# Compression of the sparse mixer with the token blocks stationary, and three modulation chunks folded during attention on GpSimd

## The chip, the cores and the metric

The kernel runs on one core of a Trainium2 chip. The metric is the device time of one execution in microseconds (us), as the median of several runs. The engines are TensorE (PE, and PEld for its weight loads), VectorE (DVE), ScalarE (ACT), GpSimd (POOL) and SyncE (SP), which issues the transfers.

## The reference, cut to what matters

The model has a two-layer transformer (the first layer with a sparse mixer, the second with differential attention), a gated delta network, and a mixture of many small experts. The change touches the sparse mixer of the first layer alone, and the modulation vector computed beside it.

```python
mod = jax.nn.silu(c) @ ada_w[i] + ada_b[i]          # c: 1024 values, mod: 6 * 1024
...
def nsa_compress(t, pos_emb, w1, w2):
    S = t.shape[2]
    ncmp = (S - NSA_CMP_LEN) // NSA_CMP_STRIDE + 1  # (256 - 32) // 16 + 1 = 15
    idx = np.arange(ncmp)[:, None] * NSA_CMP_STRIDE + np.arange(NSA_CMP_LEN)[None, :]
    blocks = t[:, :, idx] + pos_emb
    hid = jax.nn.silu(jnp.einsum('bgnld,lde->bgne', blocks, w1))
    return jnp.einsum('bgne,ed->bgnd', hid, w2)
```

For each of two key heads g there are 15 blocks of 32 tokens with 64 features d, every second block half over the one before. A block is flattened to 2048 values and multiplied by w1 (32 x 64 x 256), once for the keys and once for the values. The compressed keys are then scored against the queries, masked and put through a softmax whose rows are weighted by gates. The compressed attention is one of three branches that `sparse_attention` adds up.

## The kernel before, in words

The kernel is a row of stages. Each is a block in which every engine has its own queue of instructions, written out by hand, with semaphores between them; a barrier and the clearing of the stage's semaphores stand between two blocks. The stages around the change are `turn` (transposes of z, the projected tokens), `compress`, `sparse_attention` and `project` (the output projection).

**Weights.** w1 lies in SBUF as [128 partitions, 2 (key, value), 16, 256], fp32, 4 MB. The 128 partitions hold two tokens: 64 features of an even token l in the lower half, the same of the odd token behind it in the upper half, so that one matmul contracts two tokens. It comes in four transfers of 1 MB, two for the keys, issued by `turn` (L579) behind the positions `pos_t` and w2, and two for the values, issued by `compress` (L989).

**Compression (`compress`).** TensorE turns the tokens of both heads into `pt`, twice, into the lower and the upper 64 partitions (L1007). VectorE copies them to `tok_t` (L1074) and builds `blk` by adding the positions (L1080), even tokens for the lower half, odd ones for the upper, four additions each for key and value. TensorE then keeps a 128x128 piece of w1 stationary and moves the 30 blocks (2 heads x 15) through it: 2 (key, value) x 2 (halves of the 256 hidden values) x 16 (pairs of tokens) matmuls (L1015). An fp32 matmul of this kind shows as two records. ScalarE applies Silu from PSUM (L1053). TensorE multiplies by w2 (L1022, L1026); VectorE copies the compressed keys and values out (L1088, L1089); TensorE scores (L1035); VectorE scales and masks (L1093), takes the maximum (L1098) and subtracts it (L1099); ScalarE takes Exp (L1056); VectorE sums and weighs (L1102 to L1106); TensorE transposes the probabilities in four quarters (L1044) and VectorE copies each out (L1109).

**Modulation beside it (`Modulation`).** `mod` is built up in 24 chunks of 1 MB, one after another over several stages. A fold is one VectorE operation of 128x2048 (L178): acc = w * silu(c) + acc. Chunks 14 to 19 are loaded in this stage (L163) through two slots; the load of the third and of each later one waits until a fold has freed its slot. VectorE folds four behind the building of the blocks, one behind the copy of the compressed values, and one between the subtraction and the sum. GpSimd clears a row (L152) and does nothing else.

**Attention (`sparse_attention`).** Twelve pairs of heads go through a pipeline: TensorE scores (L1153), VectorE scales and masks from PSUM (L1204) and takes two maxima (L1209), ScalarE takes Exp and sums (L1239), VectorE takes the reciprocal (L1216), for eight pairs multiplies it by gates (L1220), and multiplies the rows in two pieces (L1222), TensorE transposes (L1163), ScalarE copies (L1247), and TensorE multiplies by the values (L1174, L1178). SyncE starts the first two tiles of the output weights at the stage's beginning (L217). GpSimd has no part.

```python
            fold(0, 4)
            dve.wait_ge(small, 1)
            ...
            dve.tensor_tensor(sc[:], sc[:], mx[:].unsqueeze(3).broadcast_to(wide), ALU.subtract).then_inc(shifted, 1)
            fold(5, 6)
            dve.wait_ge(exped, 1)
```

## Time and profile before

| what | value |
|---|---|
| median of 3 runs | 2252.08 us (2250.52 to 2254.69) |
| profiled execution, its own time | 2255.32 us |
| its span in the profile | 2253.5 us |
| compression, as a stretch of it | 137.3 to 190.7 us |
| attention of the sparse mixer | 190.7 to 236.0 us |
| busy: PE, DVE, ACT, POOL | 89%, 70%, 44%, 6% |

All times of the timeline are microseconds from the start of the span. The span is one execution; the time of the run around it is 1.8 us longer. A duration of a matmul record holds its latency, so neighbouring records overlap, and the pace is told by the time of many divided by their number. The granted clock (PEclk) is given in shares of full speed.

### The profile page before, as it was taken

The page shows a single profiled execution, that of the slowest core. Times are in us where ns is not written, and L with a number is a line of the kernel's source. Part 1 is how long each engine was busy: PE and PEld are TensorE (multiplying, and loading weights), DVE is VectorE, ACT ScalarE, POOL GpSimd, SP SyncE. Part 2 cuts the span into 40 slices and gives each one's busy share as a digit, 9 for nine tenths or more (in the row PEclk, how much of TensorE's full clock was granted, in tenths as well). Part 3 has the DMA queues.
Part 4 walks back from the last instruction along what each step waited for, and adds up shares of the span by engine and source line. Part 5 has one row for each costly group of instructions (what it writes and reads, how often), then busy time and mean ns, then how long its engine had stood idle before and what let it go on. Part 6 is the DMA issues. An engine that isn't in the chain of part 4 may idle for free. (4 is left out here: it accounts for less than half of the span.)

```text
span 2253.5 us, 40848 instructions
## 1 busy us (share of the span) xinstructions
PE 2013.6 (89%) x16472; PEld 1805.2 (80%) x16472; DVE 1570.8 (70%) x2622; ACT 1002.6 (44%) x1669; POOL 125.6 (6%) x109
## 2 busy tenths in 40 slices
PE   8877799988779996998788888899899999999996
PEld 4875599968559894878777868899899998888885
DVE  3658778867559886776566565589977776667665
ACT  2515444335553343323344553445456665454453
POOL 1000000000230001530000300000000000000000
PEclk9967999989789998998899988999999999999998
DMA  7672578835137882314000025477555555777775
GB/s 262 229 165 82 196 291 319 310 119 187 59 134 282 304 299 70 119 57 151 1 4 4 2 86 189 150 230 216 181 170 176 176 176 196 240 242 244 241 241 179
DMA packets 185264, 393.24 MB, mean 174 GB/s; under 512 B 14826, under 2 KB 130154, under 8 KB 173546
## 3 DMA queue, kind: packets, MB, share of 16 engines
q1 hardware_dynamic: 166642, 373.83, 49.1%
q10 hardware_dynamic: 18434, 16.79, 2.2%
q8 instruction: 131, 2.15, 0.4%
q14 instruction: 57, 0.47, 0.1%
HBM read 371.17 MB, written 19.40 MB: 173 GB/s over the span
## 5 line engine op out<-in xcount | busy, mean ns | idle before, releaser
L1319 ACT CAST experts_v_hi<-peer_v 128x1024 fp32r<-128x1024 f32 x128 | 134.3, 1050 | 175.8 <-PE experts_py L1309 174.7
L1516 PE MATMUL ffn_pa<-all_h_hi,ffn_u_hi 128*128 128x256 f32 x704 | 199.4, 283 | 7.1 <-DVE ffn_u_lo L1581 7.0
L1305 PE MATMUL experts_py<-experts_v_hi,experts_c_hi 128*128 128x512 f32 x512 | 200.4, 391 | 5.3 <-DVE experts_c_lo L1350 5.3
L1306 PE MATMUL experts_py<-experts_v_lo,experts_c_hi 128*128 128x512 f32 x512 | 200.1, 391 | 0.0
L1517 PE MATMUL ffn_pa<-all_h_lo,ffn_u_hi 128*128 128x256 f32 x704 | 198.2, 282 | 0.0
L1518 PE MATMUL ffn_pa<-all_h_hi,ffn_u_lo 128*128 128x256 f32 x704 | 198.2, 281 | 0.0
L1309 PE MATMUL experts_py<-experts_v_hi,experts_c_lo 128*128 128x512 f32 x512 | 158.4, 391 | 0.0
L3148 PE MATMUL table_pa<-all_h_hi,table_u_hi 128*128 128x256 f32 x512 | 151.1, 295 | 7.6 <-DVE table_u_lo L3116 7.6
L1344 DVE TENSOR_TENSOR experts_v_lo<-peer_v,experts_v_hi 128x1024 fp32r<-128x1024 f32 x128 | 155.9, 1218 | 0.6 <-ACT experts_v_hi L1319 0.6
L3070 PE MATMUL route_pa<-all_h_hi,route_u_hi 128*128 128x256 f32 x512 | 146.5, 286 | 8.8 <-DVE route_u_lo L2955 8.8
L3071 PE MATMUL route_pa<-all_h_lo,route_u_hi 128*128 128x256 f32 x512 | 145.7, 285 | 0.0
L3149 PE MATMUL table_pa<-all_h_lo,table_u_hi 128*128 128x256 f32 x512 | 145.7, 285 | 0.0
L3150 PE MATMUL table_pa<-all_h_hi,table_u_lo 128*128 128x256 f32 x512 | 145.7, 285 | 0.0
L3072 PE MATMUL route_pa<-all_h_hi,route_u_lo 128*128 128x256 f32 x512 | 145.6, 284 | 0.0
L1516 PEld LDWEIGHTS ffn_pa<-all_h_hi,ffn_u_hi 128*128 128x128 f32 x704 | 134.3, 191 | 10.9 <-DVE ffn_u_lo L1581 9.3
L1517 PEld LDWEIGHTS ffn_pa<-all_h_lo,ffn_u_hi 128*128 128x128 f32 x704 | 134.4, 191 | 1.6 <-issue 0.2
L1518 PEld LDWEIGHTS ffn_pa<-all_h_hi,ffn_u_lo 128*128 128x128 f32 x704 | 134.3, 191 | 0.0
L833 PE MATMUL proj_psum<-proj_w_hi,all_h_hi 128*128 128x256 f32 (+1 forms) x384 | 112.2, 292 | 18.4 <-DVE proj_w_lo L845 18.4
L1350 DVE TENSOR_TENSOR experts_c_lo<-experts_coef,experts_c_hi 128x256 fp32r<-128x256 f32 x128 | 54.4, 425 | 106.3 <-ACT experts_c_hi L1325 106.3
L1581 DVE TENSOR_TENSOR ffn_u_lo<-ffnw_u,ffn_u_hi 128x2048 fp32r<-128x2048 f32 (+1 forms) x50 | 101.2, 2034 | 38.7 <-ACT ffn_u_hi L1553 38.7
L1553 ACT CAST ffn_u_hi<-ffnw_u 128x2048 fp32r<-128x2048 f32 (+1 forms) x50 | 84.3, 1702 | 94.7 <-DMA ffnw_u<-in_ffn_columns 92.7
L3116 DVE TENSOR_TENSOR table_u_lo<-table_u,table_u_hi 128x1024 fp32r<-128x1024 f32 x64 | 78.5, 1227 | 63.7 <-ACT table_u_hi L3175 63.7
(586 smaller groups left out, 5828.9 us busy)
## 6 DMA issues: line engine op xcount, KB each, us to landing
peer_v<-in_peer_v SPq DMA_DIRECT2D x128, 512.0 KB, 3.4
ffnw_u<-in_ffn_columns SPq DMA_DIRECT2D x44, 1024.0 KB, 7.9
ffn_ada_w<-in_ada_w SPq DMA_DIRECT2D x40, 1024.0 KB, 5.4
route_u<-in_peer_u SPq DMA_DIRECT2D x64, 512.0 KB, 3.8
table_u<-in_peer_u SPq DMA_DIRECT2D x64, 512.0 KB, 3.3
ffnw_v<-in_ffn_rows SPq DMA_DIRECT2D x44, 512.0 KB, 8.7
peer_kept<-hid_kept SPq DMA_DIRECT2D x128, 128.0 KB, 3.4
l1w_w<-in_diff_w_in SPq DMA_DIRECT2D x12, 1024.0 KB, 5.1
```

The lines of the kernel that those rows point to most:

```text
L1305: pe.matmul(py[:, 2 * t + n, :], c_hi[:, b, part], v_hi[:, r, cols], start=start, stop=False)
L1306: pe.matmul(py[:, 2 * t + n, :], c_hi[:, b, part], v_lo[:, r, cols], start=False, stop=False)
L1309: last = pe.matmul(py[:, 2 * t + n, :], c_lo[:, b, part], v_hi[:, r, cols], start=False, stop=stop)
L1344: dve.tensor_tensor(v_lo[:, r, :], feed_v.slot(i), v_hi[:, r, :].bitcast(F32), ALU.subtract).then_inc(v_split, 1)
L1516: pe.matmul(out, u_hi[:, b, cols], h_hi[:, c, :], start=(c == 0), stop=False)
L1517: pe.matmul(out, u_hi[:, b, cols], h_lo[:, c, :], start=False, stop=False)
L1518: last = pe.matmul(out, u_lo[:, b, cols], h_hi[:, c, :], start=False, stop=(c == KT - 1))
L3070: pe.matmul(out, u_hi[:, b, cols], h_hi[:, c, :], start=(c == 0), stop=False)
L3071: pe.matmul(out, u_hi[:, b, cols], h_lo[:, c, :], start=False, stop=False)
L3148: pe.matmul(out, u_hi[:, b, cols], h_hi[:, c, :], start=(c == 0), stop=False)
L3149: pe.matmul(out, u_hi[:, b, cols], h_lo[:, c, :], start=False, stop=False)
L3150: last = pe.matmul(out, u_lo[:, b, cols], h_hi[:, c, :], start=False, stop=(c == KT - 1))
```

## The change

- The blocks are the stationary operand now, padded from 30 to 32 columns, and w1 moves, 256 columns at a time. The 16 token pairs are dealt out over four groups of 32 columns of TensorE (`l % 4`), each of which collects a partial sum in its own 32 partitions of PSUM.
- ScalarE copies the four partial sums to `part`, and two matmuls against `stack` (four 32x32 unit matrices, one below another) add them and turn the result, hidden values to the partitions. Silu reads that.
- The upper 64 partitions of `tok_t` hold the tokens shifted by one, so that both halves are read with the same pattern: two additions of 128 partitions take the place of four of 64. `pos_t` is shifted in the same way by its transfer.
- w2 is loaded behind w1 instead of ahead of it, with a semaphore of its own. Silu's table is loaded by an activation of one column (`warm`).
- VectorE's work on the gates stands behind the building of the blocks, and ScalarE makes the last four copies instead of VectorE.
- Of the six modulation chunks three stay in the compression: the first on VectorE behind the copy of the compressed values, the second on GpSimd, the third on VectorE at the very end. Chunks 17 to 19 are loaded in attention, ahead of the output weights in SyncE's queue, and folded by GpSimd. A fold on GpSimd is two operations, a multiplication in place and an addition.

```diff
+    def fold_in_two(self, pool, chunk):
+        at = chunk - self.first
...
+        pool.wait_ge(self.w_loaded[at % 2], 16 * (at // 2) + 16)
+        pool.tensor_tensor(w, w, silu_c[:, c:c + 1].broadcast_to([P, AW]), ALU.mult).then_inc(self.weighed, 1)
+        self.halfway += 1
+        pool.wait_ge(self.weighed, self.halfway)
+        if at and c:
+            pool.wait_ge(self.folded, at)
...
+        pool.tensor_tensor(acc, acc, w, ALU.add).then_inc(self.folded, 1)
 def compress(...)
         @block.sync
-            for to, of, arrived in w1_rest:
+            for to, of, arrived in transfers:
         @block.gpsimd
+            pool.memset(warm[:], 0.0).then_inc(warm_ready, 1)
             beside.zero(pool)
+            beside.fold_in_two(pool, halves[1])
         @block.tensor
-                pe.wait_ge(blk_ready, 4 * (kv + 1))
+                pe.wait_ge(blk_ready, 2 * (kv + 1))
                 pe.wait_ge(w1_loaded[kv], 32)
+                for l in range(L):
+                    rows = slice(l % 4 * GROUP, (l % 4 + 1) * GROUP)
+                    last = pe.matmul(ph[rows, kv, 0:CMP_HIDDEN], blk[:, kv, l, :], w1[:, kv, l, :], start=(l < 4),
+                                     stop=(l >= L - 4))
+                last.then_inc(e_sum, 1)
+                pe.wait_ge(part_ready, kv + 1)
                 for e in range(2):
-                    for l in range(L):
-                        last = pe.matmul(ph[:, kv, e * N:(e + 1) * N], w1[:, kv, l, e * P:(e + 1) * P],
-                                         blk[:, kv, l, :], start=(l == 0), stop=(l == L - 1))
-                    last.then_inc(e_sum, 1)
+                    last = pe.matmul(pt[kv][:, e * N:(e + 1) * N], part[:, kv, e * P:(e + 1) * P], stack[:, 0:N],
+                                     start=True, stop=True)
+                last.then_inc(joined, 1)
         @block.scalar
+            act.wait_ge(warm_ready, 1)
+            act.activation(warm[:], warm[:], ACT.Silu).then_inc(warmed, 1)
             for kv in range(2):
-                act.wait_ge(e_sum, 2 * (kv + 1))
-                act.activation(hid[:, kv].rearrange("p e n -> p (e n)"), ph[:, kv, 0:2 * N],
+                act.wait_ge(e_sum, kv + 1)
+                act.copy(part[:, kv, :], ph[:, kv, 0:CMP_HIDDEN]).then_inc(part_ready, 1)
+                act.wait_ge(joined, kv + 1)
+                act.activation(hid[:, kv].rearrange("p e n -> p (e n)"), pt[kv][:, 0:2 * N],
                                ACT.Silu).then_inc(hid_ready, 1)
...
+            for quarter in range(4):
+                act.wait_ge(p_turned, quarter + 1)
+                act.copy(pc_t[:, 2 * quarter:2 * quarter + 2, :].rearrange("n h s -> n (h s)"),
+                         pt[quarter % 2][0:NCMP, :]).then_inc(p_half, 1)
 def sparse_attention(...)
+        beside = Modulation(nc, k, st, *ada)
         @block.sync
         def _(sp):
+            for chunk in range(ada[2], ada[3]):
+                beside.load(sp, chunk)
             for feed in feeds:
                 feed.begin(sp)
+
+        @block.gpsimd
+        def _(pool):
+            for chunk in range(ada[2], ada[3]):
+                beside.fold_in_two(pool, chunk)
```

Where the folds stand is seen in the order of instructions. VectorE, compression, before: L178 is a fold, `cmp_kc_t` and `l0b_vc` are the compressed keys and values, `cmp_sc` the scores.

```order
L1080 TENSOR_TENSOR cmp_blk<-cmp_tok_t,l0b_pos_t 64x240 x4
L178 SCALAR_TENSOR_TENSOR main_mod<-cmp_ada_w,main_silu_c,main_mod 128x2048 x4
L1088 COPY cmp_kc_t<-cmp_pk 64x15 x2
L1089 COPY l0b_vc<-cmp_pv 15x128
L178 SCALAR_TENSOR_TENSOR main_mod<-cmp_ada_w,main_silu_c,main_mod 128x2048
L1093 SCALAR_TENSOR_TENSOR cmp_sc<-cmp_psc,main_cmp_mask 128x120 x2
L1098 TENSOR_REDUCE cmp_mx<-cmp_sc 128x16
L1099 TENSOR_TENSOR cmp_sc<-cmp_sc,cmp_mx 128x240
L178 SCALAR_TENSOR_TENSOR main_mod<-cmp_ada_w,main_silu_c,main_mod 128x2048
L1102 TENSOR_REDUCE cmp_sm<-cmp_sc 128x16
```

The same place of VectorE's queue now:

```order
L1113 TENSOR_TENSOR cmp_blk<-cmp_tok_t,l0b_pos_t 128x8x30 x2
L1118 TENSOR_SCALAR l0b_gates<-l0b_gates 128x48
L1119 RECIPROCAL l0b_gates<-l0b_gates 128x48
L1123 COPY cmp_kc_t<-cmp_pk 64x15 x2
L1124 COPY l0b_vc<-cmp_pv 15x128
L178 SCALAR_TENSOR_TENSOR main_mod<-cmp_ada_w,main_silu_c,main_mod 128x2048
L1128 SCALAR_TENSOR_TENSOR cmp_sc<-cmp_psc,main_cmp_mask 128x120 x2
L1133 TENSOR_REDUCE cmp_mx<-cmp_sc 128x16
L1134 TENSOR_TENSOR cmp_sc<-cmp_sc,cmp_mx 128x240
L1136 TENSOR_REDUCE cmp_sm<-cmp_sc 128x16
```

The four folds ahead of the key copy are gone, one is left between that copy and the scores, and none stands between the subtraction and the sum.

GpSimd, compression and attention, now (before, the clearing of `main_mod` was the only operation here; `ada_w` is the chunk in its slot):

```order
L1019 MEMSET cmp_warm 128x1
L152 MEMSET main_mod 128x2048
L188 TENSOR_TENSOR cmp_ada_w<-cmp_ada_w,main_silu_c 128x2048
L195 TENSOR_TENSOR main_mod<-main_mod,cmp_ada_w 128x2048
L72 UNCONDITIONAL_BRANCH
L68 ISA x24
L1179 UNCONDITIONAL_BRANCH
L188 TENSOR_TENSOR attn_ada_w<-attn_ada_w,main_silu_c 128x2048
L195 TENSOR_TENSOR main_mod<-main_mod,attn_ada_w 128x2048
```

One pair of operations stands in the compression; in attention the last two rows stand there three times.

## Rows read from the trace of the kernel before

**Rows 1.** Busy time of each engine by stretch, both stages; granted clock as PEclk

```profile
core 0: us, PE busy (x) PEld busy (x) DVE busy (x) ACT busy (x) POOL busy (x), PEclk, DMA share, GB/s
146.70:160.60 13.90, 13.86 (x66) 13.89 (x66) 0.53 (x1) 0.00 (x0) 0.00 (x0) 0.50 1.12 248
160.60:174.30 13.70, 13.62 (x64) 13.49 (x64) 8.88 (x4) 0.26 (x2) 0.00 (x0) 0.50 0.75 234
174.30:190.70 16.40, 8.90 (x48) 6.62 (x48) 10.79 (x18) 1.87 (x3) 0.00 (x0) 0.50 0.24 74
190.70:236.00 45.30, 35.42 (x280) 22.89 (x281) 37.56 (x80) 33.58 (x117) 0.00 (x0) 0.93 0.12 47
```

**Rows 2.** Timeline of the compression: start, duration, engine, line, operation, count

```profile
137.31 1.97 PE L1007 MATMUL cmp_pt<-all_ident,l0b_z 128*64 128x128 f32 x32 [0.83 <-PEq L72]
...
146.74 27.48 PE L1015 MATMUL cmp_ph<-cmp_blk,l0b_w 128*128 128x30 f32 x128 [7.46 <-DMA l0b_w<-in_cmp_w]
...
162.99 2.35 DVE L178 SCALAR_TENSOR_TENSOR main_mod<-cmp_ada_w,main_silu_c,main_mod 128x2048 f32<-128x2048 f32 x1 [0.57 <-DMA cmp_ada_w<-in_ada_w]
...
174.26 0.22 ACT L1053 ACTIVATE cmp_hid<-cmp_ph 128x60 f32<-128x60 f32 x1 [13.43 <-PE cmp_ph L1015]
...
176.16 0.37 DVE L1088 COPY cmp_kc_t<-cmp_pk 64x15 f32<-64x15 f32 x2 [2.30 <-PE cmp_pv L1026]
...
176.90 3.62 PE L1035 MATMUL cmp_psc<-cmp_kc_t,l0b_zt 128*128 128x30 f32 x16 [0.78 <-DVE l0b_vc L1089]
...
181.62 0.41 DVE L1099 TENSOR_TENSOR cmp_sc<-cmp_sc,cmp_mx 128x240 f32<-128x240 f32 x1
...
181.95 2.34 DVE L178 SCALAR_TENSOR_TENSOR main_mod<-cmp_ada_w,main_silu_c,main_mod 128x2048 f32<-128x2048 f32 x1
...
182.06 0.40 ACT L1056 ACTIVATE cmp_sc<-cmp_sc 128x240 f32<-128x240 f32 x1 [6.28 <-DVE cmp_sc L1099]
...
186.04 3.69 PE L1044 MATMUL cmp_pt<-all_ident,cmp_sc 128*15 128x128 f32 x16 [5.52 <-DVE cmp_sc L1106]
...
189.77 0.68 DVE L1109 COPY l0b_h_t<-cmp_pt 15x512 f32<-15x512 f32 x1 [0.18 <-PE cmp_pt L1044]
```

**Rows 3.** DMA into l0b_w, and issues of 120 to 192

```profile
L989 SPq DMA_DIRECT2D l0b_w<-in_cmp_w x2: 533/1342/2152, 137.3 to 137.8; - x2
DMA to landing us min/median/max: 2.1/14.0/19.4
...
cmp_ada_w<-in_ada_w SPq DMA_DIRECT2D x6, 1024.0 KB, 5.7
```

**Rows 4.** Timeline of TensorE at the end of attention

```profile
230.71 0.65 PE L1174 MATMUL attn_po<-attn_pt,l0b_z 128*64 128x256 f32 x4
```

**Rows 5.** GpSimd's groups by line: busy, mean ns of one

```profile
L1817 POOL TENSOR_TENSOR diff_w_lo<-diff_w,diff_w_hi 128x1024 fp32r<-128x1024 f32 x8 | 18.9, 2361 | 0.1
...
L2628 POOL TENSOR_TENSOR dnrec_faded<-dnrec_state,dna_exp_last 128x512 f32<-128x512 f32 x8 | 8.3, 1042 | 0.0
```

**Rows 6.** Timeline of the recurrence, VectorE and GpSimd

```profile
1270.91 1.04 POOL L2628 TENSOR_TENSOR dnrec_faded<-dnrec_state,dna_exp_last 128x512 f32<-128x512 f32 x1
...
1271.56 0.94 DVE L2685 TENSOR_TENSOR dnrec_rhs<-dnrec_bv,dnrec_rhs 128x512 f32<-128x512 f32 x1
```

**Rows 7.** Two lines of VectorE in the recurrence: min/median/max ns

```profile
L2685 DVE TENSOR_TENSOR dnrec_rhs<-dnrec_bv,dnrec_rhs x12: 691/814/943, 1266.2 to 1304.5; 128x512 f32<-128x512 f32 x12
...
L2682 DVE TENSOR_TENSOR dnrec_rhs<-dnrec_pks,dna_k_scale x12: 680/690/692, 1265.4 to 1303.7; 128x512 f32<-128x512 f32 x12
```

**Rows 8.** Timeline of VectorE in attention, one round

```profile
203.81 0.95 DVE L1204 SCALAR_TENSOR_TENSOR attn_sc<-attn_ps,main_causal 128x768 f32<-128x768 f32 x1
204.80 1.01 DVE L1209 TENSOR_REDUCE attn_nm<-attn_sc 128x2 f32<-128x256 f32 x2
205.73 0.17 DVE L1216 RECIPROCAL attn_sm<-attn_sm 128x4 f32<-128x4 f32 x1
205.93 1.02 DVE L1222 TENSOR_TENSOR attn_sc<-attn_sc,attn_sm 128x256 f32<-128x256 f32 x2
```

More of the change, by code:

```diff
@@ L1060, in _ @@
             step = InOrder(dve, dve_done)
-            def fold(first, last):
-                for n in range(first, last):
-                    beside.fold(dve, halves[n])
-            dve.wait_ge(gate_e, 1)
-            step(dve.tensor_scalar(gates[:], gates[:], 1.0, None, ALU.add))
             step(dve.memset(kc_t[:], 0.0))
-            step(dve.reciprocal(gates[:], gates[:]))
-            dve.wait_ge(small_loaded, 48)
+            step(dve.memset(blk[:, :, :, N:GROUP], 0.0))
+            step(dve.tensor_reduce(stack[:], k["ident"][:].rearrange("p (j n) -> p n j", n=GROUP), AX.X, ALU.add))
+            dve.wait_ge(small_loaded, 32)
             half = L // 2
@@ L1073, in _ @@
                 dve.wait_ge(turned, kv + 1)
-                step(dve.tensor_copy(tok_t[:, kv].rearrange("d g s -> d (g s)"), pt[kv][:]))
-                for odd, rows in enumerate(sides):
-                    steps = tok_t[rows, kv].rearrange("d g (m l o) -> d l g m o", l=half, o=2)[:, :, :, :, odd]
-                    places = pos_t[rows, kv].rearrange("d (l o) -> d l o", o=2)[:, :, odd]
-                    for m in range(2):
-                        at = slice(m * half, (m + 1) * half)
-                        dve.tensor_tensor(blk[rows, kv, at, :].rearrange("d l (g n) -> d l g n", g=G),
-                                          steps[:, :, :, m:m + NCMP],
-                                          places[:, at].unsqueeze(2).unsqueeze(3).broadcast_to([HEAD, half, G, NCMP]),
-                                          ALU.add).then_inc(blk_ready, 1)
-            fold(0, 4)
+                for g in range(G):
+                    last = dve.tensor_copy(tok_t[:, kv, g, 0:S - 1], pt[kv][:, g * S:(g + 1) * S - 1])
+                step(last)
+                steps = tok_t[:, kv].rearrange("d g (m l o) -> d l g m o", l=half, o=2)[:, :, :, :, 0]
+                places = pos_t[:, kv].rearrange("d (l o) -> d l o", o=2)[:, :, 0]
+                for m in range(2):
+                    at = slice(m * half, (m + 1) * half)
+                    dve.tensor_tensor(blk[:, kv, at, 0:N].rearrange("d l (g n) -> d l g n", g=G),
+                                      steps[:, :, :, m:m + NCMP],
+                                      places[:, at].unsqueeze(2).unsqueeze(3).broadcast_to([P, half, G, NCMP]),
+                                      ALU.add).then_inc(blk_ready, 1)
+            dve.wait_ge(gate_e, 1)
+            step(dve.tensor_scalar(gates[:], gates[:], 1.0, None, ALU.add))
+            step(dve.reciprocal(gates[:], gates[:]))
             dve.wait_ge(small, 1)
@@ L1089, in _ @@
             dve.tensor_copy(vc[:].rearrange("n g d -> n (g d)"), pv[0:NCMP, 0:G * HEAD]).then_inc(kv_ready, 1)
-            fold(4, 5)
+            beside.fold(dve, halves[0])
             dve.wait_ge(scored, 1)
@@ L1099, in _ @@
             dve.tensor_tensor(sc[:], sc[:], mx[:].unsqueeze(3).broadcast_to(wide), ALU.subtract).then_inc(shifted, 1)
-            fold(5, 6)
             dve.wait_ge(exped, 1)
@@ L1106, in _, with sparse_attention @@
             dve.tensor_tensor(sc[:], sc[:], sm[:].unsqueeze(3).broadcast_to(wide), ALU.mult).then_inc(p_ready, 1)
[L1107 to L1113 removed]
+            beside.fold(dve, halves[2])
+def sparse_attention(nc, k, z, zt, pc_t, vc, gates, o_t, feeds, ada):
     pairs = []
```

52 lines of the change are left out of this document (30 added, 22 removed).

## The prediction

> **What bounds the kernel now.** I read the page for the whole first (VectorE 70% busy, TensorE 89%), but the change touches two stages only, so the question is what ends last in each of them. Everything outside the two I leave as it is: after them the next stage starts at a barrier, and what is due there (the first two tiles of the output weights) lands early in either kernel.
>
> The table by stretches [rows 1] shows the first stage, the compression, from 137.3 to 190.7. From 146.7 to 174.3 TensorE is busy throughout (13.86 of 13.90, 13.62 of 13.70) at a granted clock of 0.50, that is at 1.2 GHz; it had been idle before, waiting for weights. The other engines have next to nothing to do there. From 174.3 to 190.7 nobody is full: 16.4 us of a chain from engine to engine. In the attention stage VectorE is busy for 37.56 of 45.3, nearly without a gap once it has started; TensorE (35.42) and ScalarE (33.58) follow it. GpSimd does nothing in either (0.00).
>
> The timeline [rows 2] gives the chain of the compression. The 128 records of the block product start at 146.74, when the first half of the weights is there, and end at 174.22: 27.48/128 = 0.215 us each. Silu ends at 174.48, the key and value copies start at 176.16, the scores end at 176.90+3.62 = 180.52, the subtraction of the maximum at 182.03. Exp is done at 182.46, but VectorE is in a fold until 184.29. The transposes start at 186.04 and the last copy ends at 190.45. The second half of the weights is not waited for: it was issued at about 137.8 and landed up to 19.4 later, 157.2 [rows 3], while the product was still on the first.
>
> **The change, part by part.** All in us of the profiled execution.
>
> *The weights.* The 128 KB of w2 go behind the 4 MB of w1 instead of ahead of them. That advances w1 by at most the 2.1 that w2 took to land [rows 3] and at least by nothing; I take 1.3, so the second half lands at 155.9. The total ahead of the modulation chunks is unchanged, so the second of these is there at 162.99 as before [rows 2]. What was hidden, the landing at 155.9, is now on the path.
>
> *The product.* Per key or value there are now 16 matmuls of 32 stationary columns and 256 moving ones: 32 records over four column groups. The nearest row is the value product of attention: 4 records of 256 moving columns over two column groups take 0.65 at the full clock [rows 4]. With 0.21 a record side by side that is two steps and the latency of the last; one after another it would be 0.85 and the latency. So two groups do run at once, and they keep it up: L1007's 32 records of 128 columns, at the full clock too, take 1.97 [rows 2], two per 0.12. For four I take 32/4 = 8 steps of 0.43 at the half clock (the engine again comes from a wait) plus 0.2: 3.6. Bounds: 1.8 at the full clock; 6.9 if only two groups run at once; 13.7 if none do. The second product ends at 155.9+3.6 = 159.5.
>
> *The joining.* New on the path: a ScalarE copy of 128x256 (as the 128x240 Exp, 0.40 [rows 2]), four records of 0.215 and their latency (1.1), then Silu (0.22) and some 0.1 of hand-over. Silu ends at 161.4 instead of 174.48: 13.1 earlier. The table load for Silu is hidden in both kernels under the wait for the weights. VectorE's block building also gets shorter, and the clearing of pads and the `stack` reduction are added, but all of it ends before 146; it costs nothing while the weights are the later.
>
> *The tail.* The fold between the subtraction and the sum goes: the sum waits for Exp (182.46) instead of the fold (184.29), and about 1.7 is gained. The four last copies go to ScalarE, as short as they were. The last fold on VectorE runs beside the transposes and needs a chunk that is loaded once the first fold is done: at 166 to 170, so it lands 5.7 later [rows 3], by 175.5 at the latest, and VectorE is then just done with the probabilities or not yet. If this were all, the stage would end at 190.45-13.1-1.7 = 175.65, **14.8 earlier**.
>
> *GpSimd beside VectorE.* This decides the sign. A fold on GpSimd is two tensor_tensor of 128x2048. The trace has it at 1.04 for 512 elements a partition and 2.36 for 1024 [rows 5]. Four times the first is 4.2, the line through both gives 5.0; I take 4.5. (Trainium skill, "GPSIMD Engine Reference", section on elementwise cycle accounting: 4497 ns for this length; the rows allow it.)
>
> Does it disturb VectorE? In the recurrence VectorE's L2685 reads two SBUF tensors. It takes 0.69 alone and 0.94 when it starts under a GpSimd tensor_tensor [rows 6, 7]: GpSimd ends at 1270.91+1.04 = 1271.95, L2685 starts at 1271.56 and ends at 1272.50, that is 0.55 after GpSimd let go. L2682, with one input in PSUM and one in SBUF, stays at 0.68 to 0.69 through the same overlaps. So an operation with two SBUF inputs seems to stand still until the GpSimd one is done. (Trainium skill, "SBUF — State Buffer", "Who interferes with whom": a two-SBUF-input VectorE instruction and a GpSimd one that reads SBUF hold each other off for the whole instruction. The trace agrees on 0.4 us of it; no row shows a wait of 4 us. By this rule the change costs time; by shared bandwidth it would not.)
>
> In the compression the second chunk lands at 162.99 and GpSimd multiplies until 167.5. VectorE would start its fold (two SBUF inputs) at 163.7; it is held to 167.5 and ends at 169.8. The scores were ready at 167.4. GpSimd's addition waits for that fold, runs to 174.3, and holds the subtraction (two SBUF inputs), due at 170.9. The subtraction ends at 174.8 instead of 169.0: **+5.8**. Had VectorE come first, it would be +5.1. The stage ends at 181.4, 9.0 earlier.
>
> In attention one round of VectorE is 3.06: mask 0.95, two reductions 1.01, reciprocal 0.17, all with at most one SBUF tensor, then two multiplications by the row factors, 1.03, with two [rows 8]. The first chunk lands 5.7 after the stage begins [rows 3], and then six operations of 4.5 stand in GpSimd's queue almost without a gap. If VectorE gets both multiplications between two of them, a round lasts 4.5+1.0 = 5.5, +2.5; six times 15, and 1 more for the first, which arrives just ahead of a pair. Where GpSimd slips in between the two, VectorE waits the full 4.5. Ends: 14 (always the pair, 4.2 each) and 25 (always between, 4.9 each); I take **+18**, nearer the lower end because the two multiplications follow each other at once. TensorE and ScalarE have slack in a stretched round, at the half clock too. SP's order is load, load, load after the first fold, then the output weights: these start some 15 after the stage begins and are needed after 60.
>
> Sum: -14.8 +5.8 +18 = **+9.0**. Against the profiled execution's own 2255.3 that is 2264; it lies 3.2 above the median of the three runs, so against that median I forecast 2261.
>
> The places in the order are the ones shown ahead: the folds that leave VectorE's queue, and the pairs in GpSimd's.
>
> **Rivals.**
> *No hold.* GpSimd and VectorE run beside each other without loss. For it: L2685 is one kind of row, with 0.4 of overlap at most, and most operations under GpSimd keep their time [rows 7]. Against it: the end of L2685 follows the end of GpSimd's. Then only the 14.8 count: 2252.1-14.8 = 2237.3, faster. It decides as soon as the hold per GpSimd operation is under about 1.5.
> *A slowdown, no standstill.* A 0.25 longer L2685 in 0.39 of overlap is also a rate of a third. Then the fold loses some 2.5 and the subtraction 0.8, and in attention five rounds lose 2 each: -14.8+3.3+10 = -1.5, 2250.6, within 0.2%.
> *The column groups run one after another.* 13.7 instead of 3.6 after the landing: the end of the chain is only 3 earlier, GpSimd's multiplication is then over before VectorE's fold, about 2 of hold are left: -3.0-1.7+2+18 = +15, 2267. The two groups of [rows 4] speak against it.
> *GpSimd always gets in between the multiplications*: +16, 2268; part of the forecast's range. With the cheap end everywhere it is -14.8+5.1+14 = +4, 2256.
>
> **Numbers.** What a measurement of this kernel can tell from no change is about 0.2%, 4.5 us. Forecast 0.59, no hold 0.21, slowdown 0.12, groups in turn 0.08. Of the forecast's 0.59 some 0.03 fall within 0.2%, of the slowdown's 0.12 about 0.02 on either side. So faster 0.23, same 0.12, slower 0.65. The forecast's own range is 2256 to 2269; for all it is 2240 to 2270, which reaches into the no-hold case until under 2 in 10 are left out.
>
> **What would show it.** L1039 should start its second half near 156 and take 3.6 (1.8 at the full clock, 6.9 or 13.7 in the rivals). The compression should end near 181.4, with L1134, two SBUF inputs, stretched from 0.41 to about 4. In attention L1261 should have single cases of 2.5 to 5, while L1243 and L1248 keep 0.95 and 0.5; the stage should be 63 long. If L1261 stays at 0.42 and 0.69 beside busy GpSimd, the forecast is wrong and the kernel faster. If the compression ends later than 185, the product or the landing was priced wrong.

## The result, and the profile after

| | before | after |
|---|---|---|
| median of 8 runs | 2252.53 us | 2263.82 us |
| lowest and highest | 2250.52 to 2256.52 | 2259.82 to 2266.4 |
| profiled execution, its own time | 2255.32 us | 2264.97 us |
| its span | 2253.5 us | 2262.8 us |

The ratio of the two kernels is 1.0044, with a 95% interval of 1.0032 to 1.0056: the change makes this kernel about 10 us slower (the two medians are 11.3 apart). The profiled executions differ by 9.65 in their own times and by 9.3 in their spans.

Over the whole span, PE's busy time fell by 20 (2013.6 to 1993.6), and DVE's rose by 8.7 (1570.8 to 1579.5) although it has fewer instructions.

The table by stretches of after, with the cuts at the places that answer to [rows 1]: the first product and the wait behind it, the second product up to the small matmuls, the rest of the compression, attention.

```profile
core 0: us, PE busy (x) PEld busy (x) DVE busy (x) ACT busy (x) POOL busy (x), PEclk, DMA share, GB/s
146.40:157.00 10.60, 4.71 (x37) 2.52 (x38) 0.00 (x0) 0.59 (x2) 0.00 (x0) 0.50 1.13 221
157.00:163.00 6.00, 5.21 (x44) 2.99 (x44) 0.00 (x0) 1.14 (x3) 0.00 (x0) 0.50 0.73 233
163.00:180.40 17.40, 8.29 (x43) 6.14 (x41) 13.20 (x14) 3.44 (x6) 8.10 (x2) 0.52 0.20 61
180.40:243.60 63.20, 39.54 (x280) 25.14 (x280) 55.34 (x80) 33.52 (x116) 25.28 (x6) 0.81 0.24 84
```

The compression is 43.4 long (137.0 to 180.4) and was 53.4. Attention is 63.2 long and was 45.3; VectorE runs the same 80 instructions in it, in 55.34 instead of 37.56, and GpSimd now has 25.28. At the start of the output projection the changed kernel is 7.6 behind (243.6 against 236.0).

The timeline of the compression after answers to [rows 2]:

```profile
146.41 3.64 PE L1039 MATMUL cmp_ph<-l0b_w,cmp_blk 128*32 128x256 f32 x32 [7.40 <-DMA l0b_w<-in_cmp_w]
...
157.00 3.64 PE L1039 MATMUL cmp_ph<-l0b_w,cmp_blk 128*32 128x256 f32 x32 [5.40 <-DMA l0b_w<-in_cmp_w]
...
162.22 0.22 ACT L1086 ACTIVATE cmp_hid<-cmp_pt 128x60 f32<-128x60 f32 x1 [1.15 <-PE cmp_pt L1044]
...
163.00 3.60 POOL L188 TENSOR_TENSOR cmp_ada_w<-cmp_ada_w,main_silu_c 128x2048 f32<-128x2048 f32 x1 [23.94 <-DMA cmp_ada_w<-in_ada_w]
...
164.80 3.94 DVE L178 SCALAR_TENSOR_TENSOR main_mod<-cmp_ada_w,main_silu_c,main_mod 128x2048 f32<-128x2048 f32 x1
...
164.93 3.62 PE L1064 MATMUL cmp_psc<-cmp_kc_t,l0b_zt 128*128 128x30 f32 x16 [0.85 <-DVE l0b_vc L1124]
...
168.90 4.50 POOL L195 TENSOR_TENSOR main_mod<-main_mod,cmp_ada_w 128x2048 f32<-128x2048 f32 x1 [2.29 <-DVE main_mod L178]
...
169.73 3.92 DVE L1134 TENSOR_TENSOR cmp_sc<-cmp_sc,cmp_mx 128x240 f32<-128x240 f32 x1
...
179.59 0.57 ACT L1092 COPY l0b_h_t<-cmp_pt 15x512 f32<-15x512 f32 x1 [0.28 <-PE cmp_pt L1073]
```

The block product is no longer 27.48 in one piece but 3.64 behind each half of the weights, and TensorE waits 5.40 for the second half: the weights' arrival is on the path. Then two operations of VectorE are held up, that is, they stand still beside a GpSimd operation; such a standstill is called a hold here. VectorE's fold (L178) starts 1.80 after GpSimd's multiplication began and takes 3.94 instead of 2.34; the subtraction (L1134) starts 0.83 after GpSimd's addition began and takes 3.92 instead of 0.41. It ends 0.25 after that addition (173.65 and 173.40).

The timeline of attention after, VectorE and GpSimd, which answers to [rows 8]:

```profile
187.37 3.60 POOL L188 TENSOR_TENSOR attn_ada_w<-attn_ada_w,main_silu_c 128x2048 f32<-128x2048 f32 x1 [13.97 <-DMA attn_ada_w<-in_ada_w]
...
188.53 7.62 DVE L1261 TENSOR_TENSOR attn_sc<-attn_sc,attn_sm 128x256 f32<-128x256 f32 x2
191.04 4.55 POOL L195 TENSOR_TENSOR main_mod<-main_mod,attn_ada_w 128x2048 f32<-128x2048 f32 x1
195.56 4.04 POOL L188 TENSOR_TENSOR attn_ada_w<-attn_ada_w,main_silu_c 128x2048 f32<-128x2048 f32 x1
...
198.18 6.62 DVE L1261 TENSOR_TENSOR attn_sc<-attn_sc,attn_sm 128x256 f32<-128x256 f32 x2
199.68 4.56 POOL L195 TENSOR_TENSOR main_mod<-main_mod,attn_ada_w 128x2048 f32<-128x2048 f32 x1
204.20 4.05 POOL L188 TENSOR_TENSOR attn_ada_w<-attn_ada_w,main_silu_c 128x2048 f32<-128x2048 f32 x1
...
206.83 6.61 DVE L1261 TENSOR_TENSOR attn_sc<-attn_sc,attn_sm 128x256 f32<-128x256 f32 x2
208.33 4.56 POOL L195 TENSOR_TENSOR main_mod<-main_mod,attn_ada_w 128x2048 f32<-128x2048 f32 x1
```

The six GpSimd operations stand one behind the other from 187.37 to 212.89. In the 26 us there are only three rounds of VectorE, and each has its pair of multiplications stretched from 1.03 to 7.62, 6.62 and 6.61. A hand-over lies inside each pair: at 191.04, 199.68 and 208.33 GpSimd's next operation starts after VectorE's first multiplication was released and before its second one has run. The excess over 1.03 is 6.59+5.59+5.58 = 17.8. The groups by line say the same for the whole stage. Before:

```profile
L1222 DVE TENSOR_TENSOR attn_sc<-attn_sc,attn_sm 128x256 f32<-128x256 f32 (+1 forms) x24 | 12.3, 555 | 0.4
```

After:

```profile
L1261 DVE TENSOR_TENSOR attn_sc<-attn_sc,attn_sm 128x256 f32<-128x256 f32 (+1 forms) x24 | 30.1, 1294 | 0.4
L1248 DVE TENSOR_REDUCE attn_nm<-attn_sc 128x2 f32<-128x256 f32 (+1 forms) x24 | 12.1, 548 | 0.4
L1243 DVE SCALAR_TENSOR_TENSOR attn_sc<-attn_ps,main_causal 128x768 f32<-128x768 f32 x12 | 11.4, 951 | 4.3 <-PE attn_ps L1192 4.3
```

One line takes 17.8 more (30.1 against 12.3), and that is the 17.9 by which the stage is longer. The mask (951 ns) and the maxima (548 ns), which run under the same GpSimd operations, keep their old pace.

### The profile page after: what moved, and what is told of

It reads as the page before. It is cut to its first block and busy times, and to the rows that moved or that the text cites. A ratio compares the mean times of both kernels' runs of the same rounds, so it can differ in the third digit from the quotient of the medians.

```text
span 2262.8 us, 40761 instructions
## 1 busy us (share of the span) xinstructions
PE 1993.6 (88%) x16416; PEld 1782.9 (79%) x16416; DVE 1579.5 (70%) x2614; ACT 1006.3 (44%) x1676; POOL 158.9 (7%) x118
## 5 line engine op out<-in xcount | busy, mean ns | idle before, releaser
L849 PE MATMUL proj_psum<-proj_w_hi,all_h_hi 128*128 128x256 f32 (+1 forms) x384 | 112.7, 293 | 17.3 <-DVE proj_w_lo L861 17.3
```

## The experiments

Two questions were open. Does the time come from the hold between GpSimd and VectorE, and if so, what about it costs the most? And how much is the compression's product on four column groups worth? Where no interval is given, the kernel ran once; the median of before on the same chip was 2253.5 to 2254.9 each time. Stage lengths are those of the profiled execution. The part of the span behind attention has the same code in all twelve kernels and is 2014 to 2021 us long in their profiled executions, so a difference of a few us between two whole times that were taken once says little.

### The folds in attention left out

```diff
-            for chunk in range(ada[2], ada[3]):
+            for chunk in range(ada[2], ada[2] + 2):
                 beside.load(sp, chunk)
+            for at in range(2):
+                sp.wait_ge(beside.w_loaded[at], 16)
...
-        @block.gpsimd
-        def _(pool):
-            for chunk in range(ada[2], ada[3]):
-                beside.fold_in_two(pool, chunk)
```

> The changed kernel without GpSimd's folds in attention; two of the three chunks are still loaded there and waited for by SyncE ahead of the output weights. It leaves chunks 17 to 19 out of the modulation vector. Hold theory (GpSimd's reads keep VectorE's two-SBUF-input operations waiting): attention back from 63.2 to 45.3 us, L1261 at 1.03 a pair in every round, the whole 17.8 shorter than the changed kernel, some 8 below the kernel before. Rival (the loads or the clock stretch attention): it stays above 55.

Measured: 2245.64, ratio 0.997 (0.9956 to 0.9984), 18.2 below the changed kernel's median where 17.8 were expected. Attention is 45.9 long, from 180.71 to 226.61, and its two multiplications are back at their old times:

```profile
L1259 DVE TENSOR_TENSOR attn_sc<-attn_sc,attn_sm x24: 424/554/686, 185.8 to 221.6; 128x256 f32<-128x256 f32 x12, 128x512 f32<-128x512 f32 x12
```

So the three folds on GpSimd cost attention 17.3, 63.2 against 45.9, and the rest of the change is a gain. This doesn't tell yet whether it is GpSimd's work, its reading, or its writing.

### GpSimd busy, but only writing

Five clearings of the slot take the place of the two operations of each chunk; the loads, the queue and the length of GpSimd's work stay.

```diff
-            for chunk in range(ada[2], ada[3]):
-                beside.fold_in_two(pool, chunk)
+            for at in range(ada[3] - ada[2]):
+                w = beside.w[:, at % 2].rearrange("p j n -> p (j n)")
+                pool.wait_ge(beside.w_loaded[at % 2], 16 * (at // 2) + 16)
+                for n in range(5):
+                    last = pool.memset(w, 0.0)
...
```

> The changed kernel with five GpSimd memsets of 128x2048 (about 1.8 us each) in place of each two-operation fold in attention, behind the same waits for the same three loads. Chunks 17 to 19 are left out of the modulation vector. GpSimd is then busy for about 27 us, as long as with the folds, but reads no SBUF tensor. Hold by reads: no VectorE operation is longer, attention 45.3 us. Rival (any GpSimd work beside VectorE costs, or its writes do): L1261 is stretched in three or more rounds, attention 55 us or more.

Measured: 2242.18 in one run, attention 45.1 (180.26 to 225.40). The timeline of GpSimd, the first of three such groups:

```profile
187.26 9.27 POOL L1185 MEMSET attn_ada_w<- 128x2048 f32 x5 [14.03 <-DMA attn_ada_w<-in_ada_w]
```

And VectorE's line of multiplications under it:

```profile
L1267 DVE TENSOR_TENSOR attn_sc<-attn_sc,attn_sm x24: 424/554/684, 186.0 to 220.4; 128x256 f32<-128x256 f32 x12, 128x512 f32<-128x512 f32 x12
```

GpSimd is busy for 27.8 here, 2.5 more than with the folds, writes a slot five times per chunk, and none of these multiplications is held (at most 684 ns). Neither the transfers nor writing by GpSimd is the cause; what is left is GpSimd's reading of SBUF. (Trainium skill, "SBUF — State Buffer", section "Who interferes with whom": a VectorE operation with two SBUF inputs contends with a GpSimd one that reads SBUF, not with one that only writes. The two traces agree, 45.1 against 63.2.)

### The GpSimd operations cut in four

Each operation of 128x2048 in attention becomes four of 128x512.

```diff
+        if self.split > 1:
+            cut = [slice(i * AW // self.split, (i + 1) * AW // self.split) for i in range(self.split)]
+            for cols in cut:
+                pool.tensor_tensor(w[:, cols], w[:, cols], silu_c[:, c:c + 1].broadcast_to([P, AW // self.split]),
+                                   ALU.mult).then_inc(self.weighed, 1)
...
+            for cols in cut[:-1]:
+                pool.tensor_tensor(acc[:, cols], acc[:, cols], w[:, cols], ALU.add).then_inc(self.weighed, 1)
...
+        beside.split = 4
```

> The changed kernel with each GpSimd operation in attention cut into four of 128x512, about 1.04 us each; same work, same reads. If a hold lasts until the end of the one GpSimd instruction, VectorE's multiplications wait at most 1 us each, two waits in a round, so about 1.5 us more a round over some five rounds: attention 52 to 55 us. If GpSimd instead slows VectorE in proportion to overlap, cutting changes nothing: attention about 63. If GpSimd keeps the port from piece to piece, also about 63 or more.

Measured: 2255.13 in one run, attention 57.4 (180.00 to 237.45), so 5.8 shorter than after, and longer than expected. The timeline, VectorE then GpSimd:

```profile
188.12 1.88 DVE L1278 TENSOR_TENSOR attn_sc<-attn_sc,attn_sm 128x256 f32<-128x256 f32 x2
...
192.03 3.16 DVE L1278 TENSOR_TENSOR attn_sc<-attn_sc,attn_sm 128x256 f32<-128x256 f32 x2
...
201.42 0.88 DVE L1276 TENSOR_TENSOR attn_sm<-attn_sm,l0b_gates 128x4 f32<-128x4 f32 x1
202.34 2.09 DVE L1278 TENSOR_TENSOR attn_sc<-attn_sc,attn_sm 128x256 f32<-128x256 f32 x2
```

```profile
187.23 4.66 POOL L192 TENSOR_TENSOR attn_ada_w<-attn_ada_w,main_silu_c 128x512 f32<-128x512 f32 x4 [14.26 <-DMA attn_ada_w<-in_ada_w]
191.97 4.35 POOL L199 TENSOR_TENSOR main_mod<-main_mod,attn_ada_w 128x512 f32<-128x512 f32 x3
```

A single hold now lasts one small GpSimd operation (the longest multiplication is 1.755 against 4.985), so its length is set by the length of the instruction on the other engine. But twice as many rounds are caught, seven instead of three, because VectorE comes by more often and GpSimd's queue lasts longer, 31.5 instead of 25.5; the tiny gate multiplication L1276 is caught too (0.88 instead of 0.16). A finer cut lessens the loss, it doesn't remove it.

### The multiplications as tensor_scalar

Whether an operation with one tensor and a column of factors escapes the hold:

```diff
-                    last = dve.tensor_tensor(sc[:, b, :, lo:hi], sc[:, b, :, lo:hi],
-                                             sm[:, b, :, t:t + 1].broadcast_to([P, 2, hi - lo]), ALU.mult)
+                    for half in range(2):
+                        last = dve.tensor_scalar(sc[:, b, half, lo:hi], sc[:, b, half, lo:hi],
+                                                 sm[:, b, half, t:t + 1], None, ALU.mult)
```

> The changed kernel with VectorE's two multiplications per round (two SBUF tensors each) written as four tensor_scalar with the row factor as a per-partition scalar: one SBUF tensor input each. Only L1259, tiny, still reads two. Hold by a second SBUF input: the multiplications are no longer held, attention about 46 to 48 us with GpSimd's folds in place. Rival (tensor_scalar from fp32 SBUF to SBUF takes both ports and is held as well): single cases of 3 to 4.5 us, attention 60 or more, perhaps longer than 63 since there are four places to slip in between.

Measured: 2263.82 in one run, attention 65.6 (180.04 to 245.67). The timeline of VectorE:

```profile
185.10 1.01 DVE L1262 TENSOR_SCALAR attn_sc<-attn_sc,attn_sm 128x128 f32<-128x128 f32 x4
...
188.14 11.08 DVE L1262 TENSOR_SCALAR attn_sc<-attn_sc,attn_sm 128x128 f32<-128x128 f32 x4
...
201.25 10.82 DVE L1262 TENSOR_SCALAR attn_sc<-attn_sc,attn_sm 128x128 f32<-128x128 f32 x4
```

The group of four is held for 10.1 and 9.8, twice. One tensor in SBUF is not what saves an operation: this form is held as the other was, and with four operations in a row more of GpSimd's get in between. The mask (one input in PSUM) and the maxima (a reduction) stay free. Why this form is held was not tested by itself; the nearest sign is the duration: 275 and 344 ns for the two shapes are less than the 424 and 684 of a tensor_tensor of twice the columns, 69 ns for 128 more columns where the tensor_tensor takes 260 for 256. It runs at about twice the pace. (Trainium skill, "SBUF — State Buffer", section "Who interferes with whom": a tensor_scalar can enter a mode that uses the port pair which VectorE shares with GpSimd, and of two operations that want the pair one is then blocked in full. The duration and the hold agree with it.)

### The three folds of attention on VectorE

```diff
-        @block.gpsimd
-        def _(pool):
-            for chunk in range(ada[2], ada[3]):
-                beside.fold_in_two(pool, chunk)
...
+                if u == 4:
+                    beside.fold(dve, ada[2])
+            for chunk in range(ada[2] + 1, ada[3]):
+                beside.fold(dve, chunk)
```

> The changed kernel with the three attention chunks folded by VectorE (2.35 us each), one after the fifth round and two behind its last multiplication, where it otherwise idles some 5 us until the stage ends; nothing on GpSimd there. Hold theory: attention 45.3 + 2.35 = 47.7 us, 15.5 below the changed kernel, about 5 below the kernel before. Rival (the last folds are not hidden): 50 to 52 us.

Measured: 2246.34, ratio 0.9969 (0.9956 to 0.9982). Attention is 49.3 long (179.38 to 228.68), 3.4 more than without folds and 1.6 more than the 47.7 expected. The same three chunks that cost 17.3 on the idle engine cost 3.4 on the busy one. The end of the stage, in its timeline:

```profile
223.60 4.81 DVE L178 SCALAR_TENSOR_TENSOR main_mod<-attn_ada_w,main_silu_c,main_mod 128x2048 f32<-128x2048 f32 x2
...
227.34 0.37 ACT L1292 COPY l0a_o_t<-attn_po 128x256 f32<-128x256 f32 x1 [1.55 <-PE attn_po L1217]
```

The last two folds run from 223.60 to 228.41 while TensorE and ScalarE still bring the last pairs to an end (227.71), so all but 0.7 of their 4.8 is covered; the one in the middle, 2.35, is paid for.

### The compression's folds on VectorE, attention as changed

```diff
-            beside.fold_in_two(pool, halves[1])
...
             step(dve.reciprocal(gates[:], gates[:]))
+            beside.fold(dve, halves[0])
...
-            beside.fold(dve, halves[0])
+            beside.fold(dve, halves[1])
```

> The changed kernel with the two early folds of the compression both on VectorE, one while it waits for the compressed keys, one behind their copy; attention as changed. Hold theory: the subtraction L1134 back from 3.92 to 0.41 us and the stage 3.6 shorter (ends near 176.5 instead of 180.2); the whole 3.6 below the changed kernel. Rival (VectorE's own fold behind the copy delays the scores' mask as much as GpSimd's did): less than 1.5 shorter.

Measured: 2257.09, ratio 1.0022 (1.0009 to 1.0034). The timeline of VectorE:

```profile
166.97 0.41 DVE L1134 TENSOR_TENSOR cmp_sc<-cmp_sc,cmp_mx 128x240 f32<-128x240 f32 x1
```

L1134 is back at 0.41, and the stage is 38 long instead of 43.4, a gain of 5.4 where 3.6 were expected; the median is 6.7 below the changed kernel's. Of the 5.4, 3.5 are the subtraction's hold. The other 1.9 were reached with a higher clock behind the wait for the weights in this execution (the second product 3.35 instead of 3.64, the 8 records of the key product 0.42 instead of 0.62) and with the weights themselves, there 0.5 earlier.

That clock would have brought next to nothing with GpSimd's fold in place. The kernel without attention's folds has the changed kernel's compression, and its profiled execution had the higher clock too (0.42 for the same 8 records; its scores end at 163.77+3.62 = 167.4). Its VectorE:

```profile
163.65 5.38 DVE L178 SCALAR_TENSOR_TENSOR main_mod<-cmp_ada_w,main_silu_c,main_mod 128x2048 f32<-128x2048 f32 x1
168.96 0.58 DVE L1128 SCALAR_TENSOR_TENSOR cmp_sc<-cmp_psc,main_cmp_mask 128x120 f32<-128x120 f32 x2
```

Counted from the stage's start the scores came 1.7 earlier than in the changed kernel, but VectorE's fold was held until GpSimd's multiplication was over and ended at 169.03, so the mask started 1.6 behind the scores and the stage was 43.2 long. The kernel with the clearings and the one with the cut operations show the same (1.4 and 1.5 behind the scores, 42.9 and 43.2 long). So the fold on GpSimd costs the compression 3.5 when the small matmuls run slowly and about 5 when they run fast. Attention, unchanged, is 63.6. Both of the change's uses of GpSimd cost time, the one in the compression a fifth to a third of the other.

### No GpSimd in either

Both of the last two edits together.

> Both of the two edits before: no fold on GpSimd anywhere, all chunks folded by VectorE, the new compression kept. If the hold is the whole cost of the change, both stages are free of it: compression ends near 176.5, attention 47.7 us, the whole 12 below the kernel before, 2241, better than either kernel. Rival (some of the loss is not the hold, such as the output projection, which lay 1.4 us longer in the changed kernel's profile): 2243 to 2247.

Measured: 2244.59 (2239.01 to 2248.12), ratio 0.9961 (0.9946 to 0.9975), so about 9 us faster than before and 19 faster than the changed kernel. That is what the rival expected (2243 to 2247) and not the 2241 of a hold that is the whole cost. It is also within the noise of the version that kept GpSimd's fold in the compression (2246.34, ratio 0.9956 to 0.9982), although its compression is 5.4 shorter in the profile (38.1 against 43.5). The table by stretches (compression, attention, and the 58 us behind it):

```profile
136.00:174.10 38.10, 18.40 (x152) 12.20 (x152) 15.10 (x28) 8.19 (x14) 1.84 (x2) 0.66 0.79 174
174.10:223.80 49.70, 36.94 (x280) 23.53 (x280) 44.44 (x83) 33.78 (x116) 0.00 (x0) 0.88 0.31 107
223.80:281.90 58.10, 45.91 (x271) 39.70 (x272) 41.93 (x51) 21.93 (x30) 5.30 (x3) 0.82 0.58 206
```

The same 58 us before and after the change:

```profile
235.90:293.90 58.00, 46.20 (x297) 38.36 (x298) 42.32 (x52) 24.99 (x34) 5.30 (x3) 0.94 0.63 227
```

```profile
243.60:301.60 58.00, 45.25 (x280) 38.21 (x281) 41.94 (x51) 23.02 (x32) 5.29 (x3) 0.88 0.60 216
```

At the start of the output projection this version is 12.1 ahead of before (223.9 against 236.0), at the end of the span 8.5. About 3.6 is given back, and 3.5 of it in the first 60 us behind attention, where the granted clock is 0.82 instead of 0.94. In after it is 0.88, and 2.0 is lost there. In the eleven other kernels of this study this stretch is longer than in before by 1.2 to 1.3 at a clock of 0.91, 1.9 to 2.6 at 0.88, 2.6 and 3.7 at 0.85 and 3.5 at 0.82. Nothing in the code of that stretch differs, so the clock is the likely cause, but that is not shown by a run of its own, and what sets the clock there was not tried.

### One column group instead of four

All 32 matmuls of a product on the same 32 columns, so that none runs beside another.

```diff
-                    rows = slice(l % 4 * GROUP, (l % 4 + 1) * GROUP)
-                    last = pe.matmul(ph[rows, kv, 0:CMP_HIDDEN], blk[:, kv, l, :], w1[:, kv, l, :], start=(l < 4),
-                                     stop=(l >= L - 4))
+                    rows = slice(0, GROUP)
+                    last = pe.matmul(ph[rows, kv, 0:CMP_HIDDEN], blk[:, kv, l, :], w1[:, kv, l, :], start=(l == 0),
+                                     stop=(l == L - 1))
...
```

> The changed kernel with all 16 token pairs of a product in one column group of 32 instead of four; the joining then reads one group. If groups run at once as the forecast took it, a product takes 13.7 us instead of 3.64 and the compression ends near 188. Rival (the product is paced by something all groups share, such as the reading of the moving weights): it takes about 3.6 to 7.

Measured: 2265.08 in one run. The timeline of TensorE:

```profile
144.85 8.91 PE L1039 MATMUL cmp_ph<-l0b_w,cmp_blk 128*32 128x256 f32 x32 [6.15 <-DMA l0b_w<-in_cmp_w]
...
156.57 7.07 PE L1039 MATMUL cmp_ph<-l0b_w,cmp_blk 128*32 128x256 f32 x32 [1.74 <-DMA l0b_w<-in_cmp_w]
...
165.02 0.42 PE L1051 MATMUL cmp_pk<-cmp_hid,l0b_w 128*64 128x15 f32 x8 [0.31 <-ACT cmp_hid L1086]
...
166.84 1.97 PE L1064 MATMUL cmp_psc<-cmp_kc_t,l0b_zt 128*128 128x30 f32 x16 [0.85 <-DVE l0b_vc L1124]
```

Its stretches (the first product, in two, the second, and what follows):

```profile
146.40:150.00 3.60, 3.60 (x13) 1.62 (x12) 0.00 (x0) 0.00 (x0) 0.00 (x0) 0.70 1.14 200
150.00:154.00 4.00, 3.76 (x18) 1.69 (x16) 0.00 (x0) 0.20 (x1) 0.00 (x0) 1.00 1.14 190
156.50:163.70 7.20, 7.07 (x32) 3.43 (x32) 0.00 (x0) 0.03 (x1) 1.12 (x1) 1.00 0.63 201
163.70:170.00 6.30, 3.56 (x36) 3.14 (x36) 3.76 (x7) 1.84 (x3) 3.28 (x2) 0.93 0.01 1
```

Two readings. First, the four groups do run at once: at the half clock four records take 0.43 together (their weight loads stand that far apart), here at the full clock one takes 7.07/32 = 0.22, which would be about the same 0.43 at the half clock. Second, the 13.7 of both the prediction and this expectation did not come, because the clock did not stay at a half: during the first product it rose (0.70 and then 1.00 by the stretches), and it was at 1.00 for the second, 7.07, and at 0.93 for the small matmuls (0.42 against 0.62) and the scores (1.97 against 3.62). Only 3.4 is lost in the second product, and 2.7 comes back in the small matmuls and the scores. The compression is 43.8 long against 43.4: between these two executions, packing the product four times as densely gained 0.4.

That comparison rests on the changed kernel's clock in its profiled execution, and other kernels with the same product had a higher one. Of the eight profiled executions on four groups, five ran the 8 records of the key product in 0.42 and three in 0.62; in the five the first half of the weights had come 7.7 to 7.9 after the stage's start, in the three 9.4 to 9.6. The scores took 3.62 in all eight, and 1.97 and 2.14 in the two kernels on one group. Why the clock of the small matmuls differs was not tried. With GpSimd's fold in the compression the faster ones gained nothing either, as shown above, since VectorE's held fold came after the scores.

### One column group, no GpSimd

> The kernel without folds on GpSimd (both stages on VectorE), and with all token pairs in one column group. In the changed kernel one group took 7 us for the second product instead of 3.64, but held the full clock until the scores were done (their 16 records 2.0 instead of 3.6), and the stage ended no later. If the clock pays the groups back, this kernel is level with the same one on four groups, 2244.6, within 3 us. Rival (that was hidden by GpSimd's hold, and the three groups are worth their 3 us once it is gone): about 3 to 4 us longer, 2248.

Measured: 2245.17, ratio 0.995 (0.9935 to 0.9966), level with the version on four groups (0.9961, 0.9946 to 0.9975). In its profiled execution the compression is 41.7 long against 38.1: the second product takes 8.63 against 3.26, and the scores give 1.5 back (2.14 against 3.62). That does not show in the medians, which are 0.6 apart. With the holds gone four groups may be worth some 3 in the stage; the whole time can't tell.

### The folds alone

The kernel before with its own product and its own order of weights; three folds stay on VectorE in the compression, chunks 17 to 19 go to GpSimd in attention.

```diff
-            fold(0, 4)
+            fold(0, 3)
...
-            fold(4, 5)
...
-            fold(5, 6)
...
+        @block.gpsimd
+        def _(pool):
+            for chunk in range(ada[2], ada[3]):
+                beside.fold_in_two(pool, chunk)
```

The lines that go and come are counted against the kernel before.

> The kernel before with the second half of the change alone: w1 stationary and the order of transfers as before, chunks 14 to 16 folded by VectorE while it waits for the first product's end, chunks 17 to 19 in attention on GpSimd as in the changed kernel. The forecast's terms: 1.7 gained between the subtraction and the sum, 17.8 lost in attention, together 16 above the kernel before, 2269. Rival (part of the 17.8 comes from the new compression, such as the clock it leaves behind): 2262 or less.

Measured: 2269.9, ratio 1.0072 (1.0053 to 1.009). Its table by stretches, compression and attention:

```profile
137.70:189.30 51.60, 37.97 (x208) 35.66 (x208) 19.80 (x32) 4.92 (x7) 1.81 (x1) 0.57 0.59 127
189.30:251.50 62.20, 39.66 (x280) 25.20 (x280) 54.32 (x80) 33.58 (x116) 25.60 (x6) 0.78 0.25 85
```

Moving folds out of the compression is worth 1.8 there (51.6 against 53.4) and costs 17 in attention (62.2 against 45.3), as the expectation had it (2269). The loss does not come from the new compression: attention is 16.9 longer without it and 17.9 with it. The new compression gains by itself, and the folds on GpSimd lose more.

## Why the prediction was right

The forecast was +9.0 on the profiled execution, and +9.65 came. Against the median of before it was 2261, in a range of 2256 to 2269, and 2263.82 came. The mechanism, GpSimd and VectorE holding each other off, is the one that the runs show. That the number lies so near is in part luck, as the parts say (and among the chances, "slower" adds up to 0.66 and not 0.65, "same" to 0.11 and not 0.12):

*The weights: wrong, 0 instead of 1.3.* The first product starts 9.4 after the stage did in both kernels (146.41-137.0 and 146.74-137.3), and the second waits until 157.00, which is 20.0 after the stage's start; in the kernel before the last transfer landed 19.9 after it (157.2). Sending the 128 KB of w2 last brought nothing that can be seen in the second half, which is the one on the path; it came 19.4 to 20.4 after the start in all ten kernels with the new order. The 1.3 was a choice between the bounds 0 and 2.1, and the lower one holds.

*The product: right.* 3.64 for 3.6, twice, at the half clock. The second ends at 160.64 instead of the 159.5 forecast, all of it from the landing. What the rival "in turn" priced at 13.7 would have been 7.07 (8.63 in the other kernel on one group): the step that failed there was to hold the clock at 0.50 for an engine that then works without a pause.

*Joining and tail: right.* The joining ends with Silu at 162.44, 1.80 behind the product (1.9 forecast). The sum starts 0.43 after the start of Exp and not behind a fold, as forecast.

*The hold in the compression: the mechanism right, the size too large (5.8 for a measured 3.7).* Forecast was that GpSimd's multiplication takes 4.5 and holds the fold so long that the scores wait. It took 3.60, the addition 4.50. The multiplication's second operand is one value per partition and the addition has two full ones; no run tells whether that makes the difference or the operation itself. So the fold ended at 168.74, 0.1 to 0.2 behind the scores (168.55), and cost nearly nothing in this execution; in the five other profiled executions with the same compression on GpSimd it cost 0.1 in two and 1.4 to 1.6 in three. The subtraction was held for 3.5. Total 3.7 instead of 5.8. With the landing 1.1 later (157.0 for 155.9) and the hold 2.1 shorter, the stage ended at 180.4 instead of 181.4.

*Attention: the size right (+17.9 for +18), the way there not as chosen.* I had taken six stretched rounds at 2.5 each, with the pair kept together, and kept "GpSimd always gets in between" as the upper end at 25. It did get in between every time. But a round that is held twice costs 5.6 to 6.6 and lasts 8.65 to 9.65, and uses up two of GpSimd's operations, so only three of them fit into GpSimd's 25.5; the upper end had taken five rounds at 4.9, which was wrong too. Three rounds at 5.9 and six at 2.5 with a little more come to nearly the same, and 18 had been chosen between the ends by a reason that did not hold (that the two multiplications stay together). The mechanism was right, the order wrong, and the size came out by luck. The cut in four shows that the loss is not fixed by the work on GpSimd: there it was 11.5 (57.4 against 45.9) for the same folds. The clearing experiment, where GpSimd is busy for longer and nothing is held, shows that it is the reading; the cut in four shows that a hold lasts for one instruction.

*What was not in the sum.* I had said that everything outside the two stages stays. The first 60 us behind attention took 2.0 more, with a lower granted clock (0.88 against 0.94), and the whole part of the span behind attention 1.7 more. It made up for the end of the compression, 1.0 earlier than forecast. In spans the sum is -10.3+17.9+1.7 = +9.3, and the rest of the 9.65 lies outside the span (2.2 around it now, 1.8 before). In twelve profiled executions that part wandered by up to 7 with the same code, so the nearness to +9.0 is chance as well.

Of the rivals, *no hold* fell with L1134 at 3.92 and L1261 at up to 4.985; *a slowdown, no standstill* with the same rows, since 0.41 of work took 3.92; *groups in turn* with 3.64 for 32 records.

The signs named ahead were all there: L1134 near 4, L1261 with single cases up to 5, L1243 at 0.95, the stage 63 long.

## What to carry to other kernels

An idle GpSimd is not free room beside VectorE: a long tensor_tensor on it stopped VectorE's operations on two SBUF tensors, and the fp32 tensor_scalar from SBUF to SBUF, until it was done, and it slipped in between two that follow each other. Before moving an elementwise step there, count what VectorE runs in that stretch by the kind of its operands; a fold of 2.35 on VectorE, put where the other engines still finish (0.7 of two folds showed), was far cheaper than 8.2 on GpSimd. And when a matmul stage is packed more densely, compare the whole stage and not the product: here a product 3.4 shorter was worth 0.4 in one pair of executions and one 5.4 shorter 3.6 in another, because the small matmuls behind it ran at a lower clock and another engine's hold could end later than they did.

## What the runs showed of the hardware that was not expected

- A GpSimd tensor_tensor of 128x2048 in fp32 takes 3.60 as a multiplication by a broadcast column, and 4.49 to 4.56 as an addition of two full operands.
- The hold works both ways. GpSimd's multiplication takes 4.04 to 4.05 instead of 3.60 when it starts just as VectorE's second multiplication gets its turn.
- A waiting GpSimd operation gets in between two VectorE operations that stand back to back: it did so in all twelve pairs that uncut folds held in four kernels, 6.61 to 6.62 for the pair in nine of them and 6.93 to 7.62 in three, where the first was caught early.
- Clearing by GpSimd, at 1.85 for 128x2048, doesn't hold VectorE at all.
- A tensor_scalar from SBUF to SBUF is held (up to 4.58) although it reads one tensor.
- Behind the product on four column groups the scores ran at the half clock in all eight profiled executions (3.62 for 16 records). Behind the same product on one group, in which TensorE had no pause, they took 1.97 and 2.14 in two; in the first of these the clock was 1.00 in the second product.
